# Gate products between attention steps, two-pass scores and PV, and the convolution LayerNorm beside the gates, in a decoder layer

## The reference

```
z = x @ w_in
q, k, v, f, glu_a, glu_g, sc_b, sc_c, sc_h = split(z)
c = cumsum(log_sigmoid(f + b_forget))                  # per head
br_att  = softmax(q k^T / 8 + c_i - c_j, causal) @ v   # 8 heads of 64
u       = causal_conv31(glu_a * sigmoid(glu_g)) + conv_b
br_conv = silu(layer_norm(u, conv_ln_g, conv_ln_b))
br_sc   = sc_b * causal_conv3(sc_c * sc_h)
merged  = sum_n sigmoid(x @ w_gate[n] + b_gate[n]) * (br[n] @ w_branch[n])
x = layer_norm(alpha * x + merged @ w_out)
x = layer_norm(alpha * x + moe(x))       # 32 experts in 8 groups, top 2 of the best group
```

## Time and profile before

| | us |
|---|---|
| median of 3 runs | 1892.18 (1891.51 to 1895.94) |
| the profiled execution | 1892.34 |
| its span, first to last instruction | 1890.7 |
| projection, with its first product | 20.9 to 400.3 |
| forget chain, LayerNorm, first loads | 400.3 to 440.9 |
| attention | 440.9 to 674 |
| first gate chunk's way in | 674 to 679 |
| gates and branches | 679 to 1073 |
| output projection and router | 1073 to 1198 |
| routing on DVE | 1198 to 1242 |
| experts and last LayerNorm | 1242 to 1890.7 |

### The profile page before, as it was taken

How to read it: one execution, slowest core, us unless ns; L and a number is a source line. 1 busy time by engine, 2 the same in 40 slices (tenths; PEclk the granted TensorE clock), 3 DMA queues, 4 the chain that set the end, 5 groups by cost and what they waited for, 6 DMA issues and landing times.

```text
span 1890.7 us, 24894 instructions
## 1 busy us (share of the span) xinstructions
PE 1667.9 (88%) x7934; PEld 1376.1 (73%) x7934; DVE 1161.7 (61%) x1312; ACT 838.0 (44%) x1091; POOL 200.4 (11%) x181
## 2 busy tenths in 40 slices
PE   7999999965877879999999899379999999999981
PEld 5878787854666668888888788258887777777771
DVE  2747474864667621132232455669988888888884
ACT  3121212153555521121221311148888787878775
POOL 0000000001101000000000022112122222222220
PEclk9999999986999989999999999679999999999995
DMA  4122214312011011411211272329999999999975
GB/s 136 41 61 43 60 49 51 51 45 59 23 35 23 0 50 50 139 50 44 95 50 45 63 274 112 123 102 388 383 365 370 363 361 356 362 363 367 361 263 191
DMA packets 155320, 300.89 MB, mean 159 GB/s; under 512 B 17453, under 2 KB 91181, under 8 KB 155288
## 3 DMA queue, kind: packets, MB, share of 16 engines
q1 hardware_dynamic: 144648, 279.36, 42.7%
q0 software_dynamic: 10640, 21.13, 4.2%
HBM read 277.75 MB, written 33.69 MB: 165 GB/s over the span
## 4 chain that ended last, share of the span: by engine, by line
PE 58%; DMA 23%; DVE 9%; ACT 6%; issue 3%; POOL 0%; SPq 0%; ACTq 0%; POOLq 0%; DVEq 0%
PE ps L552 44%; DMA e_raw<-in_w_down 21%; PE ps L755 6%; PE ps L643 3%; DVE e_lo L1412 2%; PE ps L631 2%; ACT e_hi L988 1%; DVE pt_lo L1172 1%; DVE rmax L1156 1%; DMA x_d<-x 1%; ACT pt_hi L871 1%; PE ps L722 1%; DVE prob L1166 1%; ACT zsq L1048 1%; DVE wo_lo L1198 0%
## 5 line engine op out<-in xcount | busy, mean ns | idle before, releaser
L1412 DVE TENSOR_TENSOR e_lo<-e_raw,e_hi 128x1024 fp32r<-128x1024 f32 x376 | 442.5, 1220 | 62.9 <-ACT e_hi L988 58.5
L988 ACT ACTIVATE e_hi<-e_raw 128x1024 fp32r<-128x1024 f32 x376 | 383.8, 1057 | 88.6 <-DMA e_raw<-in_w_down 66.0
L552 PE MATMUL ps<-xt_hi,w_hi 128*128 128x512 f32 x896 | 279.6, 394 | 16.8 <-DVE w_lo L1119 11.6
L552 PE MATMUL ps<-xt_lo,w_hi 128*128 128x512 f32 x896 | 278.8, 393 | 0.0
L552 PE MATMUL ps<-xt_hi,w_lo 128*128 128x512 f32 x896 | 278.1, 392 | 0.0
L552 PEld LDWEIGHTS ps<-xt_hi,w_hi 128*128 128x128 f32 x896 | 169.9, 190 | 53.6 <-DVE w_lo L1119 12.9
L552 PEld LDWEIGHTS ps<-xt_lo,w_hi 128*128 128x128 f32 x896 | 170.1, 190 | 35.8
L552 PEld LDWEIGHTS ps<-xt_hi,w_lo 128*128 128x128 f32 x896 | 169.8, 190 | 35.7
L1202 DVE TENSOR_TENSOR w_lo<-w_raw,w_hi 128x512 fp32r<-128x512 f32 x72 | 47.5, 687 | 225.1 <-ACT w_hi L915 225.1
L755 PE MATMUL ps<-e_hi,xe_hi 128*128 128x512 f32 x512 | 165.0, 404 | 22.9 <-DVE e_lo L1412 20.6
L1128 DVE SCALAR_TENSOR_TENSOR conv<-upad,cols,conv 128x1024 f32 x120 | 153.9, 1282 | 12.2 <-DVE conv L1126 0.2
(11 more groups left out here) (254 smaller groups left out, 2578.7 us busy)
## 6 DMA issues: line engine op xcount, KB each, us to landing
e_raw<-in_w_up SPq DMA_DIRECT2D x248, 512.0 KB, 15.1
e_raw<-in_w_down SPq DMA_DIRECT2D x128, 512.0 KB, 15.8
w_raw<-in_w_in SPq DMA_DIRECT2D x64, 256.0 KB, 4.9
w_raw<-in_w_gate SPq DMA_DIRECT2D x48, 256.0 KB, 3.0
w_raw<-in_w_branch SPq DMA_DIRECT2D x24, 256.0 KB, 2.8
x_raw<-in_x SPq DMA_DIRECT2D x8, 512.0 KB, 7.4
qk_raw<-qkv SPq DMA_DIRECT2D x16, 256.0 KB
wo_raw<-in_w_out SPq DMA_DIRECT2D x8, 512.0 KB, 7.3
```

The source lines that it names most:

```text
L552: last = nc.tensor.matmul(o(h, c1 - c0), st(k), mv(k, c0, c1), start=start and k == nk[0] and n == 0, stop=h in stop and k == nk[-1] and n ...
L988: nc.scalar.activation(e_hi[:, (UPT + s) % RSPL, :], e_raw[:, s, :], ACT.Copy).then_inc(e_h, 1)
L1412: nc.vector.tensor_tensor(e_lo[:, sp_, :], e_raw[:, s, :], e_hi[:, sp_, :], ALU.subtract).then_inc(e_all, 1)
```

## The change

- **Attention takes gate products.** The gate products of branches 1 and 2 (32 chunks) are made between the attention steps: `gate_half` issues 12 matmuls in each of the 64 steps. ACT applies the gate's function to `gate_t`, POOL stores the tile to `gates_d`, and SP loads it again when its branch is merged.
- **Two passes.** Scores use stacked operands of 128 rows: `q_dup` (q high twice) x `k_two` (k high over k low), then `q_low` (q low and forget rows) x `k_aug` (k high and forget rows). PV multiplies the probabilities' high and low parts with V's high and low parts stacked in 128 columns (`v_two`); ACT copies one half of the result (`o_half`) and DVE adds the other (`output`).
- **Order of the blocks.** The query blocks go in `ORDER` (7, 0, 6, 1, 5, 2, 4, 3). Odd steps have one PSUM bank for their scores, even steps two, and banks 6 and 7 hold the gates.
- **Forget chain and first head.** The forget chain stands behind pass 0 of the projection, on ACT and DVE; the split of the first head's q and k behind pass 2. The projection, the attention and the gate stage are no loops any more but written out. q, k and v go through `qkv_d`, stored by POOL.
- **LayerNorm beside gates.** What is left of the gate stage is a list `STREAM` of 40 chunks: 16 gate chunks of branch 0 and 24 branch chunks. The transposes of the convolution LayerNorm stand behind branch chunks 0, 1, 3 and 4.
- **Gates by tanh.** sigmoid(a) = 0.5 (1 + tanh(a/2)): ACT computes tanh, `merge` adds 1 in the same DVE instruction that multiplies, and the 0.5 goes into the split of `merged`.
- **Tail.** W_out is split beside branch 1's chunks; the twelve first expert loads are issued two at a time behind the stores of the token tiles.

```diff
+CB = CT * NCH
+GT = 2 * KT
+CC = CB + 2 * GT
+ORDER = (7, 0, 6, 1, 5, 2, 4, 3)
+PAIRED = {2: 0, 3: 1, 6: 2, 7: 3}
+AUG = DH + 4
+STREAM = [("g", 0, 0), ("g", 0, 1), ("g", 1, 0), ("g", 1, 1), ("b", 0, 0)]
+for _i in range(2, KT):
+    STREAM += [("g", _i, 0), ("g", _i, 1), ("b", _i - 1, 0)]
+STREAM += [("b", _t, 0) for _t in range(KT - 1, NBR * KT)]
+CE = CC + len(STREAM)
+POS = {_w: CC + _p for _p, _w in enumerate(STREAM)}
...
-            for s in range(XT):
-                load(s, s, w_up[0, 1, s * P:(s + 1) * P, :] if s < UPT else w_down[0, 0, (s - UPT) * P:(s - UPT + 1) * P, :])
-
+            sp.wait_ge(merge_ok, NBR * KT)
             for t in range(TT):
                 if t + 2 < TT:
                     sp.wait_ge(y1_ok, t + 1)
                     sp.dma_start(x_res[t % 2][:], x[0, (t + 2) * P:(t + 3) * P, :]).then_inc(xres_in[t % 2], 16)
                 sp.wait_ge(x1_ok, t + 1)
                 sp.dma_start(x1_d[t * P:(t + 1) * P, :], x1[:]).then_inc(x1_out, 16)
+                if t < XT // 2:
+                    for s in (2 * t, 2 * t + 1):
+                        load(s, s, w_up[0, 1, s * P:(s + 1) * P, :] if s < UPT else w_down[0, 0, (s - UPT) * P:(s - UPT + 1) * P, :])
...
+            def split_qk(h):
+                u = h % 2
+                pool.wait_ge(qk_h, 3 * h + 2)
+                nc.gpsimd.tensor_tensor(k_two[u][DH:P, :], k_raw[DH:P, :], k_two[u][DH:P, :], ALU.subtract).then_inc(qk_l, 1)
+                nc.gpsimd.tensor_tensor(q_low[u][0:DH, :], q_raw[0:DH, :], q_dup[u][0:DH, :], ALU.subtract).then_inc(qk_l, 1)
...
+            def store_gate(m):
+                pool.wait_ge(tanh_ok, 2 * m + 4)
+                pool.dma_start(gates_d[m], gate_t[:, m % 2, :]).then_inc(gate_out[m % 2], 16)
...
+            for i in range(CT):
+                if i == 1:
+                    pool.wait_ge(f_dve, 6)
...
+                store_qkv(i)
+                pool.wait_ge(conv_chain, (i + 1) * CONV_LINKS)
+                pool.dma_start(conv_d[i * P:(i + 1) * P, :], conv[:, i, :]).then_inc(conv_out, 16)
+                if i == 2:
+                    pool.wait_ge(forget_out, 128)
+                    load_aug(0)
+                    split_qk(0)
+            pool.wait_ge(qkv_out, 16 * 3 * (CT - 1))
+            load_aug(1)
+
+            for n in range(STEPS):
+                if n % TT == 0 and 2 <= n // TT + 1 < HEADS:
+                    load_aug(n // TT + 1)
+                if n % 4 == 1 and n >= 4:
+                    store_gate(n // 4 - 1)
+                if n % TT == 3 and n // TT + 1 < HEADS:
+                    split_qk(n // TT + 1)
+            store_gate(GT - 1)
+
...
+            def scores(n):
+
+                head, r = n // TT, ORDER[n % TT]
+                u, nk, m0 = head % 2, nkeys(r) * P, r * P
+                if n % TT == 0:
+                    pe.wait_ge(qk_h, 3 * (head + 1))
+                    pe.wait_ge(qk_l, 2 * (head + 1))
+                    pe.wait_ge(aug_in[u], 32 * (head // 2 + 1))
+                if n >= 2:
                     pe.wait_ge(exp_ok, n - 1)
-                b = 2 * (g % 2)
...
-                product(lambda h, n: ps[:, b + h, 0:n],
-                        [(lambda k, q=q: q[:, u, 0, r * P:(r + 1) * P], lambda k, a, e, v=v: v[:, u, 1, a:e])
-                         for q, v in ((qk_hi, qk_hi), (qk_hi, qk_lo), (qk_lo, qk_hi))],
+                product(lambda h, w: out[:, h * HALF:h * HALF + w],
+                        [(lambda k, q=q: q[u][:, m0:m0 + P], lambda k, a, e, v=v: v[u][:, a:e])
+                         for q, v in ((q_dup, k_two), (q_low, k_aug))],
                         [0], cut, True, [h for h, _, _ in cut if h != m0 // HALF])
...
                 for k in range(nk):
-                    for n, (v, p) in enumerate(((v_hi, pt_hi), (v_hi, pt_lo), (v_lo, pt_hi))):
-                        last = nc.tensor.matmul(ps[:, 6, 0:2 * P], v[:, k, :], p[:, t // 2 % 2, k, :],
-                                                start=k == 0 and n == 0, stop=k == nk - 1 and n == PASSES - 1)
+                    v = v_two[:, k, 2 * u:2 * u + 2, :].rearrange("p b d -> p (b d)")
+                    for s, p in enumerate((pt_hi, pt_lo)):
+                        last = nc.tensor.matmul(o_bank(j), v, p[n % 2][:, k, :], start=k == 0 and s == 0, stop=k == nk - 1 and s == 1)
                 last.then_inc(o_ok, 1)
...
+            def gate_half(n):
+
+                m, h, j = n // 4, n % 4 // 2, n % 2
+                c = CB + 2 * m + j
+                if h == 0:
+                    pe.wait_ge(lo_ok, c + 1 + RING)
+                if j == 0:
+                    pe.wait_ge(tanh_ok, 2 * m + h + 1)
+                last = product(lambda _, w: ps[:, 6 + h, :],
+                               [(lambda k, w=w: w[:, c % RING, k - j * KC, :], lambda k, a, b, v=v: v[:, k, a:b])
+                                for w, v in ((w_hi, xt_hi), (w_hi, xt_lo), (w_lo, xt_hi))],
+                               range(j * KC, (j + 1) * KC), (HALVES[h],), j == 0, (h,) if j else ())
+                if h == 1:
+                    last.then_inc(w_used, 1)
+                elif j == 1:
+                    last.then_inc(g_mm, 1)
+
+            pe.wait_ge(f_act, 1)
+            for n in range(STEPS):
+                scores(n)
+                if n >= 2:
+                    transpose_p(n - 2)
+                if n >= 3 and (n - 3) % TT in PAIRED:
+                    attend(n - 3)
+                if n % (2 * TT) in (1, 3):
+                    transpose_v(n // (2 * TT), 1 if n % (2 * TT) == 1 else 0)
+                gate_half(n)
+
...
+            for kind, j, half in STREAM[2:]:
+                if kind == "g":
+                    gate_mm(j, half)
+                else:
+                    branch_mm(j)
+                    if j < 2:
+                        for t in range(4 * j, 4 * j + 4):
+                            ln_in(t)
+                    if j in (3, 4):
+                        for t in range(4 * (j - 3), 4 * (j - 3) + 4):
+                            ln_out(t)
...
+            for i in range(CT):
                 for c in range(NCH):
-                    act.wait_ge(raw_in[c % RING], i * (16 * NCH // RING) + 16 * (c // RING + 1))
-                    act.wait_ge(w_used, i * NCH + c + 1)
-                    nc.scalar.activation(w_hi[:, c % RING], w_raw[:, c % RING], ACT.Copy).then_inc(hi_ok, 1)
+                    split_w(i * NCH + c)
                     if c >= 3 and c % 2 == 1:
                         take_out(i, (c - 3) // 2)
-                take_out(i, len(KINDS) - 1)
...
+                if i < CT - 1:
+                    take_out(i, len(KINDS) - 1)
+                if i == 0:
+                    forget()
+                if i == 2:
+                    act.wait_ge(forget_out, 128)
+                    for part in range(3):
+                        split_qk(0, part)
+            split_w(CB)
+            split_w(CB + 1)
+            take_out(CT - 1, len(KINDS) - 1)
...
+            def split_pt(n):
+                r = ORDER[n % TT]
+                act.wait_ge(t_ok, n + 1)
+                if n == 0:
+                    act.wait_ge(conv_out, 16 * CT)
+                nc.scalar.activation(pt_hi[n % 2][:, 0:nkeys(r), (r % 2) * P:(r % 2 + 1) * P], tiles(4)[:, 0:nkeys(r), :],
                                      ACT.Copy).then_inc(pt_h, 1)
...
+                b = ROW_BGATE * CT + (m // KT + 1) * 2 * CT + m % KT
+                nc.scalar.activation(gate_t[:, m % 2, h * HALF:(h + 1) * HALF], ps[:, 6 + h, :], ACT.Tanh, scale=0.5,
+                                     bias=cols[:].rearrange("p r j -> p (r j)")[:, b:b + 1]).then_inc(tanh_ok, 1)
+
+            for n in range(STEPS + 2):
+                i, g, m, q = n // (2 * TT), n % (2 * TT), n // 4, n % 4
+                if n >= 2:
+                    split_pt(n - 2)
+                if n < STEPS:
+                    exponential(n)
+                if n >= 3 and (n - 3) % TT in PAIRED:
+                    output(n - 3)
+                if n < STEPS and g in (1, 3):
+                    split_v(i, 1 if g == 1 else 0)
+                if n < STEPS and q == 2:
+                    gate_tanh(m, 0)
+                if q == 0 and m >= 1:
+                    gate_tanh(m - 1, 1)
+                if n < STEPS and q < 2:
+                    split_w(CB + 2 * (m + 1) + q)
+                if 1 <= n % TT <= 3 and n // TT + 1 < HEADS:
+                    split_qk(n // TT + 1, n % TT - 1)
...
+                if i == 0:
+                    forget()
+            split_w(CB)
+            split_w(CB + 1)
...
+            for n in range(STEPS + 2):
+                i, g, m, q = n // (2 * TT), n % (2 * TT), n // 4, n % 4
+                if n < STEPS:
+                    maximum(n)
+                if n >= 2:
+                    split_pt(n - 2)
+                if n < STEPS:
+                    normalize(n)
+                if n >= 3 and (n - 3) % TT in PAIRED:
+                    output(n - 3)
```

(34 more changed lines are left out.)

757 lines of the change are left out of this document (402 added, 355 removed).

## The result

The changed kernel takes 1758.5 us (median of 4 runs, 1754.8 to 1759.2) against 1891.9 us before (1889.9 to 1895.9): a ratio of 0.9289, 95% interval 0.9268 to 0.9309. Its profiled execution took 1758.4 us with a span of 1756.7. The forecast was 1757, span 1755.2. So the span came out within 1.5 us.

What follows compares the result with a forecast made beforehand. Attention was taken as bound by the way round over ACT and DVE, leaving idle time for gate products. 1890.7 less 132.7 (up to the gate stage's end) and 2.8 (output projection) gave span 1755.2, forecast 1757 us, range 1742 to 1800.

Steps and rivals of the forecast that it cites:

- What bounds the kernel: Attention is held by the way round from the transposes over ACT and DVE, not by any engine's work.
- Gate halves cover it: In attention, 175.1 us of gate products fill TensorE's waits; TensorE's work there sums to 291 us.
- The allowance of 8 us: Added to the whole attention stage for waits at odd places, such as V's split; bounds 0 and 50.6.
- Forget chain behind pass 0: In the projection, the chain ahead of the next splits makes a TensorE gap of 16.2 us, 12.3 more than before.
- Clock behind the long gap: In the projection, slower products after the 16 us gap cost 1.8 us; bounds 0 and 6.5.
- Start: The first projection product was taken to start at 20.87 us, as before.
- Gate stage: 40 remaining chunks at 5.47 us plus 64 LayerNorm transposes take 225.3 us; branch products wait only for an earlier merge.
- Output projection: Gap before its first matmul falls to 4.3 us, spread expert loads bring 0.8, W_out's late splits 0.6; together 2.8.
- Expert stage: From 1242 us to the end nothing changes; it only starts earlier. Another time than 648 us would show the prediction wrong.
- the four: Rivals: gate halves do not cover (1799 us, 0.13), DVE behind POOL (1783, 0.13), slow code supply (1929, 0.03), no net change (0.01).
- The supply of the written-out code: Rival: unrolled matmuls are supplied too slowly up to the gate stage's end; at 0.04 us each, 1929 us; chance 0.03.
- A delay of VectorE by GpSimd: Rival: in attention POOL's subtractions hold up a DVE normalisation once a head, costing 34 us, 1783 us; chance 0.13.

Runs made afterwards that it cites:

- gates_behind: The changed kernel with all 64 gate halves (products, tanh, splits, loads, stores) behind the 64 attention steps instead of between them; 1859.6 us, ratio 0.985.
- pv_twice: The changed kernel with one extra PV product for each of the 160 key tiles, overwritten by the real products; 1775.0 us, ratio 0.940.
- start_wide: ends_open with input transposes going round four pairs of PSUM banks instead of two; 1720.1 us, ratio 0.910.
- ends_open: The changed kernel with the forget chain, v's take-out and the first head's q and k splits moved from pass ends behind later splits; 1724.2 us, ratio 0.912.

## Why the prediction was right

- **What bounds the kernel** (the way round in attention, not an engine): right. gates_behind keeps that way and the new products, and stays at 224 us for the steps.
- **Gate halves cover it**: right. The allowance of 8 us and the 1 us at the start of attention were not needed at all; TensorE never waited. Its own work was put at 291 us and is 296.8, 5.8 too little. 4 of these are in the small instructions that I lumped at 41 us: in the chain the 320 transposes of P take 35.3, the 32 of V 3.5 and the 64 mask matmuls 6.3, 45 in all (eight transposes take 0.87 us, 0.109 each where I took 0.10). The other 2 are in the scores and gate products. With the 9 us of allowance that were not needed the term was 3.2 us too much.
- **Forget chain behind pass 0**: 16.2 told, 16.7 measured. The gap behind pass 1: 2.6 and 2.5. Behind pass 2: 5.8 and 6.5; the queue there was right, and the rest is `w_lo` behind GpSimd, which the prediction gave to a rival at up to 2.3 us: 1.16 measured.
- **Clock behind the long gap**, +1.8: a term that was counted twice. The sum starts from the old end of the projection, 400.3, and the 0.2317 us a product of the earlier trace rows already had the slow microseconds behind the old gaps in it; at a steady clock it is 0.228. Each of the three new gaps has 1.6 to 2 us of slower products behind it (88.95 against 87.33), the long one no more than a short one, and 1.0 us less than the old gap at the same place (88.96 against 89.98). No run comes near the bound of 6.5.
- **Start**: I took 20.87 as fixed. It was 22.5 us here, 22.3 to 22.7 in four of the other kernels with this start and 21.5 in pv_twice. Of the 1.65 us, 0.5 are a first transpose at 5.02 instead of 4.52, and some 0.9 the slow transposes of the third and fourth tile (see start_wide); why they were slow in five kernels and not in two stays open. The late start hid the clock's double count.
- **Gate stage**: 225.3 told, 226.5 measured. The one wait is 1.4 us, ahead of the last product of branch 0. I had written that a branch product waits only for the merge two before it. That holds for branches 1 and 2; the products of branch 0 share one pair of banks, and the last two of them stand next to each other in `STREAM`, so the second waits for a `merged` of 1.23 us.
- **Output projection**: the gap 4.3 told, 4.38 measured (the earlier trace rows had 5.68); the stage in all 0.2 off. How much of it the order of the expert loads brought (0.8 told) and what W_out's splits cost (0.6 told, from no row) was not taken apart.
- **Expert stage**: "only starts earlier", 648.5 us. It was 651.7. The text named this as a way to be wrong, and it was: 1.3 us are the first block (14.0 against 12.73 in the earlier trace rows), which depends on the clock at which it starts, and 2.0 lie behind it and stay open.
- **Rivals**: none of the four came. The supply of the written-out code would have shown in the pace; the four passes of it ran at 0.228 us a product without a break in ends_open. A delay of VectorE by GpSimd exists, and cost 1.2 us where no slack stood before TensorE and nothing elsewhere: in the attention the normalisations of 256 columns take 0.87 us in the mean where they took 0.35 before, and TensorE never waits.

The errors sum: +1.65 start, +1.1 gaps, -1.8 clock, -1.0 since the old pass 1 had been a microsecond longer than the new one, -3.2 attention, +1.2 gates, +0.2 output projection, +3.2 experts: 1.4 in all, which with rounding is the 1.5 measured. Without their signs they are 13.

## What to carry to other kernels

When every engine is partly idle and waits go round a loop of engines, fewer instructions on one of them bring little (9 us of 26 here), while independent work put into the same in-order lists can run in the idle time (here all of it: 102.6 us less for the two together, and TensorE never waited); once the lists are full, each instruction saved counts again. At the end of a phase look at what stands in the program order of the helper engines between the last product and the next operand: here a few moved calls were worth 32 us up to the attention, near a quarter of what the whole change brought. Price a gap with the slower clock behind it, and take the pace of a product from a stretch that has no gap in it.

## What was not expected of the hardware

- A gap of 2.5 us on TensorE left the clock at 1.00 once and brought it to 0.68 once, in the same run and between the same instructions; a gap of 16.7 us cost no more behind it than the one that brought it to 0.68.
- 64 table loads of 1.28 us on ScalarE, 82 us, cost TensorE 4.4 us.
- A VectorE subtraction with two SBUF operands took 2.47 us instead of 0.69 because GpSimd's had started 0.46 us before it; GpSimd's next one took 2.72 instead of 2.39.
- Idle TensorE kept busy with products that nobody reads shortened the real ones behind it by 2.8 us, and the kernel by about 3.
